# Feed-forward "up" projections in a two-layer trunk: fourteen block products per pair of units, W12 added by transfer, W21 kept on chip

## The reference, cut to what matters

```python
def swiglu(h, w_gate, w_up, w_down):
    return (jax.nn.silu(h @ w_gate) * (h @ w_up)) @ w_down

for layer in range(DEPTH):
    ...
    h = rms_norm(x, ffn_norm[layer])
    x = x + swiglu(h, w_gate[layer], w_up[layer], w_down[layer])
```

## Time and profile before

| | before |
|---|---|
| median of three runs | 1890.61 us |
| the profiled execution | 1890.08 us |
| its span (first to last instruction) | 1888.3 us |
| TensorE busy | 1879.0 us |
| VectorE busy | 1528.4 us |
| ScalarE busy | 1000.2 us |
| feed-forward of layer 0 | from 463.5 us to about 1138 us |
| feed-forward of layer 1 | from 1187.3 us to the end |

### The profile page before, as it was taken

One profiled execution on the slowest core, in us unless ns is written; L12 is line 12 of the kernel. 1 busy time (PEld: TensorE's weight loads), 2 busy tenths in 40 slices (PEclk: granted clock), 3 DMA queues, 4 the chain that ended last, 5 costly groups with the idle time before them and its releaser, 6 DMA issues.

```text
span 1888.3 us, 22147 instructions
## 1 busy us (share of the span) xinstructions
PE 1879.0 (100%) x9142; PEld 1583.5 (84%) x9142; DVE 1528.4 (81%) x1139; ACT 1000.2 (53%) x771; POOL 80.0 (4%) x125
## 2 busy tenths in 40 slices
PE   9999999999999999999999999999999999999998
PEld 8889999988888888888888888888888888888886
DVE  6656788966699899898897757889989899898855
ACT  6444344445555565555554536756565565555534
POOL 1000000000000000001000400010000000000000
PEclk9999999999999999999999999999999999999999
DMA  9555445355697868878878755497986868868762
GB/s 305 194 175 174 146 155 161 140 190 167 195 286 246 231 223 266 254 250 221 278 223 239 249 203 179 161 229 256 261 287 226 228 223 263 251 249 235 246 228 89
DMA packets 231772, 414.49 MB, mean 220 GB/s; under 512 B 6449, under 2 KB 55682, under 8 KB 231426
## 3 DMA queue, kind: packets, MB, share of 16 engines
q1 hardware_dynamic: 210336, 370.71, 56.3%
q0 software_dynamic: 21120, 41.95, 13.2%
q10 hardware_dynamic: 226, 0.55, 0.1%
HBM read 411.08 MB, written 2.10 MB: 219 GB/s over the span
## 4 chain that ended last, share of the span: by engine, by line
PE 97%; DVE 1%; DMA 1%; ACT 0%; issue 0%; SPq 0%; DVEq 0%; ACTq 0%
PE main L1844 28%; PE main L1850 14%; PE aux L1866 11%; PE main L1786 8%; PE main L1866 7%; PE aux L1870 6%; PE main L1788 4%; PE main L1870 3%; PE main L2083 3%; PE aux L2083 3%; PE main L2089 2%; PE aux L2089 1%; PE aux L1961 1%; PE aux L1793 1%; PE main L1894 1%; PE main L1893 1%
## 5 line engine op out<-in xcount | busy, mean ns | idle before, releaser
L807 ACT CAST hi<-raw 128x2048 fp32r<-128x2048 f32 (+1 forms) x328 | 624.5, 1907 | 503.1 <-PE main L1850 227.6
L1173 DVE TENSOR_TENSOR lo<-raw,hi 128x2048 fp32r<-128x2048 f32 x255 | 581.1, 2288 | 119.6 <-ACT hi L807 119.5
L1844 PE MATMUL main<-hi,mid 128*128 128x512 f32 x1632 | 387.8, 390 | 0.5 <-ACT hi L807 0.5
L1844 PEld LDWEIGHTS main<-hi,mid 128*128 128x128 f32 x1632 | 305.5, 188 | 63.9 <-issue 0.9
L807 ACT CAST hi<-work 128x2048 fp32r<-128x2048 f32 (+2 forms) x102 | 191.2, 1877 | 145.7 <-PE main L1850 26.6
L1173 DVE TENSOR_TENSOR lo<-work,hi 128x2048 fp32r<-128x2048 f32 x97 | 221.6, 2286 | 43.7 <-ACT hi L807 43.7
L1786 PE MATMUL main<-act,hi 128*128 128x512 f32 x640 | 226.6, 397 | 0.0
L1165 DVE TENSOR_TENSOR lo<-raw,hi 128x2048 fp32r<-128x2048 f32 x71 | 162.4, 2290 | 71.8 <-ACT hi L807 71.8
L1850 PE MATMUL main<-lo,mid 128*128 128x512 f32 x816 | 201.6, 389 | 0.0
L1850 PEld LDWEIGHTS main<-lo,mid 128*128 128x128 f32 x816 | 153.2, 188 | 31.8
L1788 PE MATMUL main<-act,lo 128*128 128x256 f32 x640 | 178.5, 279 | 0.0
(11 more groups left out here) (210 smaller groups left out, 2295.8 us busy)
## 6 DMA issues: line engine op xcount, KB each, us to landing
raw<-in_ffn_w_up SPq DMA_DIRECT2D x73, 1024.0 KB, 5.9
raw<-in_ffn_w_gate SPq DMA_DIRECT2D x63, 1024.0 KB, 7.0
raw<-in_ffn_w_down SPq DMA_DIRECT2D x58, 1024.0 KB, 6.6
raw<-in_ab_w_in SPq DMA_DIRECT2D x55, 1024.0 KB, 5.1
raw<-in_ffn_w_gate POOLq DMA_DIRECT2D x31, 1024.0 KB, 9.1
work<-in_ffn_w_down SPq DMA_DIRECT2D x30, 1024.0 KB, 7.5
work<-in_ffn_w_gate SPq DMA_DIRECT2D x25, 1024.0 KB, 8.0
work<-in_ffn_w_up SPq DMA_DIRECT2D x23, 1024.0 KB, 7.5
```

The source lines that it names most:

```text
L807: return nc.scalar.copy(out_, in_)
L1173: V.tensor_tensor(lo[:, split_at(t), :], raw_of[p.at], hi[:, split_at(t), :].bitcast(F32), ALU.subtract).then_inc(lo_ready, 1)
L1844: mm(o2[:, h, :], lhs[:, k0 + n, c, h * P:(h + 1) * P], w_hi, start=(first and c == 0 and n == 0), stop=False)
```

## The change

The up of every group is done in fourteen products like the gate: u0 to u5 and z0 for the first K range, y0 to y5 and z1 for the second. q, r, u6, v and w no longer stand in the orders. W12 reaches the ups' sums by accumulating transfers too (`ADDED_BY_DMA`). The last sum of weights is made on top of W11 (`add(w11, w21)`), so that W21 stays in its place until both its uses are done: x0, x1, z0 and z1 read the block that was loaded for step 5. The second turn of a group goes to other banks than the first and no longer waits until the first is taken. The orders are new; in `FIRST` the products of the gate now start between the slots of unit 0. Counted per layer: 174 slots become 192; of them 77 + 21 = 98 products become 140, and 76 wide slots become 52. Outside the feed-forward stage nothing changes.

```diff
-FIRST = ("g0 g1 g2 g3 h0 h1 h2 h3 a0 T0 a2 b0 e0 a1 b2 e1 b1 a3 a4 e2 b3 a5 b5 x0 x1 b4 e3 u2 r0 u0 q0 "
-         "u1 u6 u3 q1 u4 u5 r1").split()
-MIDDLE = ("T0 a0 a2 T1 b0 b2 d00 d01 a1 x0 d10 b1 d11 a4 d20 a3 a5 x1 b3 d21 b5 b4 d30 d31 u0 u2 q0 u1 "
-          "q1 u6 u3 r0 u5 u4 r1").split()
-LAST = ("T0 a0 a2 T1 b0 b2 d00 a1 d01 a3 a5 d10 d11 b1 x0 d20 a4 d21 x1 b3 b4 b5 d30 v0 d31 v1 w0 v2 "
-        "v3 w1 t0 w2 w3 D00 t1 D10 D01 D11 D20 D21 D30 D31").split()
+FIRST = ("g0 g1 g2 g3 a0 h0 a2 a1 b0 b2 h1 a3 x0 a5 a4 b1 h2 h3 x1 T0 b3 u0 b5 b4 e0 y0 u1 u2 u3 e1 z0 "
+         "u5 y1 y2 y3 e2 u4 z1 y5 e3 y4").split()
+MIDDLE = ("a0 b0 T0 T1 x0 a2 d00 a1 d01 a3 b2 a5 a4 b1 d10 x1 b3 d11 u0 b4 b5 d20 y0 u1 u2 u3 y2 d21 u5 "
+          "y1 z0 u4 z1 y3 d30 y5 y4 d31").split()
+LAST = ("a0 b0 T0 T1 x0 a2 a1 d00 a3 b2 a5 b1 x1 b3 d01 b5 u0 a4 y0 b4 d10 d11 u1 u2 u3 z0 u5 z1 y2 "
+        "y1 u4 y3 d20 y5 d21 y4 d30 t0 d31 t1 D00 D10 D01 D11 D20 D21 D30 D31").split()
...
-GATE_OPS, GATE_SIGS, UP_OPS, LAST_UP_OPS = 7, 4, 12, 4
+GATE_OPS, GATE_SIGS = 7, 4
+UP_OPS = {"full": 11, "half": 12, "plain": 4}
...
-ADDED_BY_DMA = ("a", "b")
-SOURCE = {k: "002025" if k in ADDED_BY_DMA else "0020W5" for k in "abu"}
+ADDED_BY_DMA = ("a", "b", "u", "y")
+W21_STAYS = True
+SOURCE = {k: "002" + ("02" if k in ADDED_BY_DMA else "0W") + ("0" if W21_STAYS else "5") for k in "abuy"}
+RAW_W21 = {"x0": "a5", "x1": "b5", "z0": "u5", "z1": "y5", "u6": "u5"}
+W21_IN = {"a": ("x0",), "b": ("x1",), "u": ("z0", "u6"), "y": ("z1",)}
...
                     ve.wait_ge(sum_made, SUMS[g.pair, k, 3])
-                    add(w21, w11)
+                    if W21_STAYS:
+                        add(w11, w21)
+                    else:
+                        add(w21, w11)
...
+                def full_ups(g, s):
...
+                    if s == due[0]:
+                        used(g, "y3", "y0")
...
+                        minus(kept_b, bank_q6, kept_a).then_inc(up_ready, 1)
+                    if s == due[1]:
+                        used(g, "z1")
...
+                        plus(kept_a, kept_a, bank_x).then_inc(up_ready, 1)
...
+                        scaled(g00, kept_a, norm, 0, g00).then_inc(up_ready, 1)
...
-                            take_hidden(layer, 0 if t.first else t.a - 2 + i, i, bank_b)
+                            take_hidden(layer, 0 if t.first else t.a - 2 + i, i, bank_a if i else bank_b)
...
-            def turn_wide(k, src, o=None):
-
-                need(pe, turn_taken, k)
+            def turn_wide(k, src, o=None, ahead=0):
+
+                need(pe, turn_taken, k - ahead)
...
                     elif g.first:
                         pe.wait_ge(a_ready, 2 * layer + 1)
-                        pe.wait_ge(job_emptied, g.j - 1)
+                        if i in (3, 4):
+                            pe.wait_ge(job_emptied, g.j - 1)
+                    elif i in (3, 4):
+                        pe.wait_ge(turn_taken, T_HIDDEN[layer] + g.a)
+                        pe.wait_ge(up_ready, g.before.up0 + (1 if i == 3 else 5))
+                    elif g.before.ups == "full":
+                        pe.wait_ge(up_ready, g.before.up0 + (2, 11, 9, 1, 5, 7)[i])
...
+                    if g.ups == "full":
+                        product(s, banks_full[i], operand(0, i), True, False)
...
-                        pe.wait_ge(up_ready, t.before.up0 + (8 if i == 0 else 12))
-                        turn_hidden(layer, t.a - 2 + i, i, bank_b)
+                        pe.wait_ge(job_emptied, t.before.j + 4)
+                        pe.wait_ge(up_ready, t.before.up0 + (8 if i == 0 else UP_OPS[t.before.ups]))
+                        turn_hidden(layer, t.a - 2 + i, i, bank_a if i else bank_b, i)
...
+                    elif kind == "y":
+                        product(s, banks_full[i], operand(1, i), False, True)
+                    elif kind == "z":
+                        if i == 0:
+                            pe.wait_ge(up_kept, g.nth("u0") + 1)
+                        product(s, bank_x, a_tiles(2 * i + 1, 0), i == 0, i == 1)
```

More of the change, by code:

```diff
@@ L122, in pair, with earlier, nth @@
         return PAIRS_OF_UNITS * self.layer + self.n
-    def nth(self, k):
-        return self.ups if k == "u" else self.pair
     @property
     def ups(self):
-        return (PAIRS_OF_UNITS - 1) * self.layer + self.n
+        return "full" if "y0" in self.at else "half" if "u0" in self.at else "plain"
+    @property
+    def earlier(self):
+        return [g for groups in LAYERS for g in groups if g.pair < self.pair]
+    def nth(self, step):
+        return sum(step in g.at for g in self.earlier)
     @property
     def up0(self):
-        return UP_OPS * self.ups + LAST_UP_OPS * self.layer
+        return sum(UP_OPS[g.ups] for g in self.earlier)
     @property
@@ L160, in up_due @@
         since = self.gate_due[-1]
-        if self.final:
+        if self.ups == "full":
+            return self.due(("u3", "y3", "y0"), ("z1", "x1"), (), ("u1", "y1"), ("u4", "y4"), (), ("u5", "y5"), (),
+                            ("u2", "y2"), (), (), since=since)
+        if self.ups == "plain":
             return self.due(("v3",), (), ("w3",), (), since=since)
@@ L196, in block_of @@
 def block_of(step):
-    return step[0] if step[0] in "abu" and int(step[1:]) < BLOCK else None
+    return step[0] if step[0] in "abuy" and int(step[1:]) < BLOCK else None
 SLOT_OF = {s: (g, step) for steps in STEPS for g, step, s, _ in steps}
@@ L262, in places @@
                 continue
-            take(s, last_use(g, step, s), layer)
+            loads = loaded_at(step)
+            if g.at[loads] not in out:
+                take(g.at[loads], last_use(g, loads, s), layer)
             if w12_loaded(step):
@@ L275, in place_of @@
     if k is None:
-        return PLACES[g.at[step]]
+        return PLACES[g.at[loaded_at(step)]]
     source = SOURCE[k][int(step[1])]
@@ L648, in _, with place @@
                         load(Count(s0 + 2 * m + i), wide_rows(ab_w_out[0], row + WIDE * i, WIDE * m), 4)
-            def place(p, src, layer=0):
+            def place(p, src, layer=1):
                 if p.fresh:
@@ L657, in block_of_w, with load_step @@
                 return wide_rows(w, WIDE * row, WIDE * u)
-            def load_step(layer, g, step, s):
+            loaded = set()
+            def load_step(layer, g, step):
+                step = loaded_at(step)
+                s = g.at[step]
+                if s in loaded:
+                    return
+                loaded.add(s)
                 kind, i = step[0], int(step[-1])
@@ L680, in load_step @@
                 elif kind in "vw":
-                    place(p, block_of_w(w, i, g.a + (kind == "w")))
+                    place(p, block_of_w(w, i, g.a + (kind == "w")), layer)
                 elif kind == "e":
@@ L686, in load_step @@
                 else:
-                    place(p, wide_rows(w_down[layer], WIDE * (g.a + i), WIDE * int(step[1])))
+                    place(p, wide_rows(w_down[layer], WIDE * (g.a + i), WIDE * int(step[1])), layer)
             for layer, steps in enumerate(STEPS):
@@ L693, in _ @@
                 for g, step, s, _ in steps:
-                    load_step(layer, g, step, s)
+                    load_step(layer, g, step)
                     if step == "D01":
@@ L1103, in keep_products @@
                         copy(kept_a, bank_x).then_inc(p1_kept, 1)
-                    if step == "u0":
+                    if step == ("y0" if g.ups == "full" else "u0"):
                         sc.wait_ge(slot_used, s + 1)
@@ L1108, in keep_products @@
                         copy(kept_a, bank_x).then_inc(up_kept, 1)
-                    if not g.final and s == g.up_due[7] + 1:
+                    if g.ups == "half" and s == g.up_due[7] + 1:
                         sc.wait_ge(up_ready, g.up0 + 8)
@@ L1720, in _ @@
                     gates(g, s)
-                    (last_ups if g.final else ups)(g, s)
+                    {"full": full_ups, "half": ups, "plain": last_ups}[g.ups](g, s)
                     if step[0] == "e":
@@ L2154, in up_product @@
                         pe.wait_ge(gate_ready, g.ready("p7"))
-                    product(s, banks_u[i], a_tiles(1, 0) if i == 6 else operand(0, i), i < 5,
-                            i in (0, 1, 3, 4) or (i > 4 and s > g.at["q1"]))
+                    elif i == 5 and g.ups == "full":
+                        pe.wait_ge(gate_ready, g.ready("g01"))
+                    if g.ups == "full":
+                        product(s, banks_full[i], operand(0, i), True, False)
+                    else:
+                        product(s, banks_u[i], a_tiles(1, 0) if i == 6 else operand(0, i), i < 5,
+                                i in (0, 1, 3, 4) or (i > 4 and s > g.at["q1"]))
                 def down(g, step, s):
```

106 lines of the change are left out of this document (72 added, 34 removed).

## The result

The changed kernel takes 1861.62 us (median of 4 runs, 1860.43 to 1862.33) against 1890.55 us before (4 runs): a ratio of 0.9847, 95% interval 0.9835 to 0.9858. Forecast were 1859.0 us and 1856.5 to 1874. The profiled execution took 1860.43 us, its span is 1858.7 us, 29.6 us less than before; twelve products are 32.6.

What follows compares the result with a forecast made beforehand. TensorE, busy for all of the span, was taken as the bound: 1890.1 - 32.6 (twelve products) + 0.5 (bursts) + 1.0 (start of a layer) = 1859.0 us, with a range of 1856.5 to 1874.

Steps and rivals of the forecast that it cites:

- TensorE loses 12 products, 32.6 us: Feed-forward stages: 6 products fewer per layer, over two layers 12 x 2.72 = 32.6 us less TensorE time.
- VectorE 115.5 us per middle group, 95%: Middle groups: VectorE's work comes to 115.5 us beside TensorE's 121.5, going from 89% busy to 95%.
- Bursts and layer start, 1.5 us: Runs of products where VectorE falls behind, put at 0.5 us, and the start of a layer, put at 1 us.
- Moved waits ... All nothing: Waits at the turns and x0, now for residual add or bank copy: no cost, covered by 0.9 us and more.
- h1 of layer 1: FIRST in layer 1: block ready at 1232.0, TensorE there at 1231.6; 0.4 us, up to 3, put at 1 us.
- Accumulates cost 0: Eight accumulating transfers per group instead of four: all spares, 11.9 us and up, exceed the slowest landing of 11.0; cost 0.
- rival 4: Slower: accumulates back up in their own queue, 6.55 us apiece; landings at 16.5 us would give 1915 us; chance 0.05.
- The prices for late landings: Accumulates landing at L us cost what exceeds their spares: per layer 3.9 us at L = 14, 8.1 at 15, 20.4 at 16.
- DMA at 91%: Middle group: 20 loads and 8 accumulates take 111 of 121.5 us of DMA time, 91% instead of 80%.
- Rival 1: VectorE becomes the bound at 95% busy: 30 us at worst over 10 groups, some 15 as middle value, 1874 us; chance 0.13.
- rival 3: DMA queues take turns, so accumulates beside loads take twice 6.55 us and land in 15.5: 1887 us; chance 0.03.
- It doesn't do what it says: Rival: for instance the place planner makes loads wait so that nothing is gained, 1890 us; chance 0.03.

Runs made afterwards that it cites:

- the run gave 48.5: Against the changed kernel, GpSimd makes 20 small waited-for settings ahead of each accumulating transfer, 3.5 us later: 1910.1 us, 48.5 us slower.
- The run at 94%: Against the changed kernel, with its new orders, W21 is loaded again instead of kept: 1923.8 us, 62 us slower.

## Why the prediction was right

- **TensorE loses 12 products, 32.6 us.** Right: 144 matmuls fewer, middle groups of 121.5 us as worked out, and the last group's products worth 2.7 us each.
- **VectorE 115.5 us per middle group, 95%.** Measured 116.7, 96%, 1.2 us more than the sum, and it hides as said. Its total rose by 97.4 us (97 forecast).
- **Bursts and layer start, 1.5 us.** Measured 2.9. The step that failed is "Moved waits ... All nothing": it was checked for MIDDLE, where d31 stands between y4 and the turns, and FIRST ends with y4, so the second turn waits 0.78 us per layer. h1 of layer 1, for which 1 us stood, waited for nothing: TensorE reached it at 1216.95, its cast began at 1214.02. The wait at u2 came as located, 0.5 and 0.3 us, though the burst was not its only cause; that of b0 in layer 1, 0.5 us, was not foreseen. That the sum still came within 2.6 us of the result is in part luck: these terms are all small, and the largest of them stood for a wait that did not come.
- **Accumulates cost 0.** Nearly right (up to 0.3 us of the wait at u2 in each layer is theirs), with less margin than was said. The step "each is over the 11.0 of the slowest landing" took the landings as staying there, and 17 of 80 went past it: in FIRST u0's took 12.7 us against a spare of 12.7, in the middle group 12.7 against 14.6, and FIRST's pair 14.8, where the spare is 20. The landings of 14 us and more, each close behind another accumulate, are what rival 4 describes, and they fell where spares were large; those of 12 to 13 us follow no other so closely. The prices for late landings failed as well: for 13.3 us instead of 9.8 the prediction's sum is 4 us in two layers, the run gave 48.5. Each transfer was charged only with what exceeds its own spare, in which 2.76 us of VectorE's lateness counted as free each time; at 96% VectorE cannot make up a wait, so the waits of a group add up and share 4 us.
- **DMA at 91%.** Measured 89%; an accumulate took 6.1 us of DMA time (eight took 40.2% of 121.5 us), not 6.55. The run at 94% lost 62 us, but places changed in it too, so it does not show where the edge of the DMA engines lies.
- **Rival 1** (VectorE the bound) did not occur but was close: 2.9 us more work for VectorE in a middle group (119.6 instead of 116.7) cost 20 us in all. The queues do take turns, as rival 3 says: the trace has 258 packets of each in the same 4 us. But its price, twice 6.55 us, was mis-sized: a load's packet takes about half as long as an accumulate's (39.0% against 71.0% of the engines' time for the same number), and loads are not always there. The landings have a median of 9.8 us, not 15.5.
- **"It doesn't do what it says"** looked only at the orders. The runs show what carries the change: taking away the kept W21 loses 62 us, the own banks 53 and the new orders 90 (1952.1 - 1861.6), of which the twelve products are 32.6. These losses overlap and do not add up.

## What to carry to other kernels

Where one engine is 100% busy and a second reaches 96%, the second's idle time is a budget for the whole group: add up all its waits against it, instead of asking of each transfer whether it is in time. A change that keeps blocks longer in shared places has to be judged with the order of the loads; the same edit lost 45 us in one order and was needed in the other. And check a cover at the seams between hand-written lists, not only inside the one that repeats.

## What the runs showed of the hardware

- A wait of TensorE of 4.0 us was followed by some 6 us of work at a granted clock of 0.50, which cost 3 us more. Of two shorter waits in one run, 2.46 us was followed by none of it, and 2.07 us by sixteen matmuls in 5.53 us instead of 3.79.
- Two accumulating transfers issued 2 us apart took 8.7 and 14.8 us to land, and a pair in layer 1 10.6 and 16.5: the second landed 8.1 and 7.8 us after the first. The eight of a middle group took 8.5 to 12.7 us.
- Where accumulates and loads move together, both queues move 64 packets in a us, and accumulates alone 100.
- With loads and accumulates at 94% of the DMA engines' time instead of 89%, loads took a median of 7.6 us to land instead of 6.6.
